# Seven chunks of a fourth output unit ahead of the first stage's last chunk, and the last attention shares turned after three chunks instead of six

## The chip, the cores and the metric

The kernel runs on one core of one Trainium2 chip. The metric is the device time of one execution in microseconds; the lower the better. All times below that name a place in the execution are microseconds from the start of the profiled span.

## The reference, cut to what matters

Two transformer-like blocks follow each other on a sequence of 512 positions with 1024 channels in float32. The change touches the end of the first block's mixing stage and the end of the second block's attention.

```python
# first block, one of 8 heads each for the recurrence (y_a) and the stick-breaking attention (y_b)
y_a = rg_lru(conv(xr), ...) * gelu(yr)
y_b = stick_breaking_attention(q, k, v)
mix = sigmoid(ga) * y_a + sigmoid(gb) * y_b      # [512, 1024]: 8 chunks of 128 channels, one a head
x = x + gt1 * (mix @ w_out)                      # 8 output units of 128 channels, each over 8 chunks
h2 = rmsnorm(x, norm2_g) * (1 + sc2) + sh2       # needs the sum of squares over all 1024 channels
# second block, latent attention, 8 heads
p = softmax(q @ k.T); o = p @ v                  # p is "the shares", 4 blocks of 128 queries
x = x + concat([o, pooled]) * silu(gate) @ w_out # a_out units: the half that reads o
```

## The kernel before, in words

Activations lie transposed: 128 channels on the partitions, 512 positions along the row. A *unit* is 128 output channels: up to eight chunks of 128 input channels, and three matmuls of 128x128 weights by 512 columns for each chunk (high weights by high input, high by low, low by high), since each float32 value is split into two parts, "hi" and "lo". `unit(kind, m, hi, lo, part=range(...))` issues some chunks of a unit on TensorE; the function starts at L715, and its three matmuls are L729 to L731.

Weights of a unit arrive by DMA in one of three `raw` buffers (L574). ScalarE copies them to the home's hi half (L1262, one instruction), and GpSimd subtracts to make the lo half in two instructions (L690, L695), after which the semaphore `w_split` is raised. There are three ordinary homes and two or three spare ones at a time. A home is used again only when the unit that read it before is finished (`unit_done`). Among the units of the first stage's output, `w_out` 0, 1 and 2 lie in ordinary homes 2, 0 and 1; `w_out` 3 and 4 in the two spare homes (seen in the trace as `qk_hl`); `w_out` 5, 6 and 7 take the homes of `w_out` 0, 1 and 2 again; then `ff_g` 0 takes that of `w_out` 3, `ff_v` 0 that of `w_out` 4, and `ff_g` 1 that of `w_out` 5.

TensorE's program is one list in a fixed order. At the end of the first stage it is: the gates of head 7, the turned weights of its attention (L898), `w_out` 0 over seven chunks, the attention products (`products`, L905), `w_out` 1 and 2 over seven chunks, then a wait for the eighth mixed chunk (`y_mixed`, raised by VectorE at L1984), the eighth chunk's matmuls for units 0 to 2 by the hi input (L993), then by the lo input (L997, after `mixed`, L1986), which finish these three units, and then units 3 to 6 whole. Unit 7 is done in two halves of 256 columns (L1016 to L1018). In its second half, before chunk 3, TensorE waits for the summed squares and turns them into a sum over channels:

```python
if i and k == 3:
    pe.wait_ge(x_summed, SUMS[0] + 6)
    nc.tensor.matmul(m_a[:, HALVES[0]], c_("ones"), sq_sum[:, HALVES[0]], start=True, stop=False)   # L1011
```

The squares come about as follows. VectorE adds a finished unit to `x` (L2059), ScalarE squares it (L1331), GpSimd adds the square to `sq_sum` (L651). ScalarE's program for this stretch is

```python
for m in range(7):
    split_ahead(UNIT[("w_out", m if m < 6 else 7)])   # L1262 for every home that is free by then
    act.wait_ge(res1_done, m + 1)
    x_square(0, m)                                    # L1331
```

and GpSimd's is in a fixed order too: the lo halves of `w_out` 5 and `w_out` 6, add 1, `w_out` 7, add 2, `ff_g` 0, add 3, `ff_v` 0, add 4, `ff_g` 1, add 5, add 6, `ff_v` 1. The lo half of `w_out` 5 can't begin before ScalarE has written its hi half, and that waits for the home of `w_out` 0 (L1257).

After the sum (L1011 and L1013) ScalarE takes the root (L1278, L1281), VectorE scales (L2073), ScalarE and VectorE make `h` hi and lo, and the next stage's first three units begin on TensorE (`trio`, L806 to L811).

At the end of the second attention TensorE runs `a_out` 0 over six chunks, the products of head 6, `a_out` 1 over six chunks, and then turns the four blocks of head 7's shares (`shares_turned(g, b)`, L1111, four transposes each). A block goes through one of two banks of PSUM; ScalarE copies it out (L1652) and VectorE subtracts (L2345, raises `pt_low`). `shares_turned(g, b)` waits for `pt_low` of the block two before it, and for the shares themselves (`p_ready`, GpSimd, L679). Between the blocks stand the seventh chunk of `a_out` 0 and of `a_out` 1. The seventh chunk of `a_out` 0 waits for `ya_tail` (VectorE, L2338).

Of the kernel before, what the change touches and what calls it, by code (L numbers as in the profile page):

```python
# [208 lines left out]
def build(nc, ada, weights, c_rows, params, consts, rg_w, x_t, positions, inv_counts, out_t):  # L209
    ctx = ExitStack()  # L210
    with ctx:
# [219 lines left out]
        def c_(name):  # L431
            a, n = CONST[name]
            return cst[:, a:a + n]
# [97 lines left out]
        def weights_of(n):  # L531

            hi, lo = home(PACK[n])
            cols = slice(WCOL[n], WCOL[n] + P * UNITS[n][2])
            return hi[:, cols], lo[:, cols]

        def psum_of(n):
            if BANK[n] > 4:
                return m_b
            return lin[:, BANK[n], :] if BANK[n] < 2 else big[:, BANK[n] - 2, :]  # L540
# [14 lines left out]
        def freed(n):  # L555
            kind, j, _ = UNITS[BEFORE[n]]
            return FREED[kind], 4 if kind == "ckv" else j + 1
# [156 lines left out]
        def _(pe):  # L714
            def unit(kind, j, hi, lo, ready=None, part=None):  # L715

                n = UNIT[(kind, j)]
                nk = UNITS[n][2]
                w_h, w_l = weights_of(n)
                if part is None or part[0] == 0:  # L720
                    pe.wait_ge(w_split, PACK[n] + 1)
                    if BEFORE[n] is not None:
                        f, v = freed(n)
                        pe.wait_ge(f, v)
                for k in part or range(nk):
                    if ready:
                        pe.wait_ge(*ready(k))
                    wh, wl = w_h[:, k * P:(k + 1) * P], w_l[:, k * P:(k + 1) * P]
                    nc.tensor.matmul(psum_of(n), wh, hi(k), start=(k == 0), stop=False)  # L729
                    nc.tensor.matmul(psum_of(n), wh, lo(k), start=False, stop=False)  # L730
                    last = nc.tensor.matmul(psum_of(n), wl, hi(k), start=False, stop=(k == nk - 1))  # L731
                if k == nk - 1:
                    last.then_inc(unit_done, 1)
# [22 lines left out]
            def YH(k):  # L756
                return y_hi[:, k]

            def YL(k):
                return y_lo[:, k]  # L760
# [130 lines left out]
            def weights_turned(g):  # L891

                pe.wait_ge(att_exp, g + 1)
                for of_bank in ((0,), (1, 3), (2,)):
                    for j in of_bank:
                        for b in range(j, TB):
                            to, of = COL[j] + (b - j) * P, COL[TB - 1 - b] + j * P
                            last = nc.tensor.transpose(big_f[:, to:to + P], att_a[:, of:of + P], c_("ident"))  # L898
                    last.then_inc(att_turned, 1)

            def products(g):

                for j in range(TB):
                    pe.wait_ge(att_done, 3 * g + (1, 2, 3, 2)[j])
                    last = nc.tensor.matmul(m_o[:, j * P:T], vtok[:, g % 2, j],  # L905
                                            att_b[:, COL[j]:COL[j] + KW[j]],
                                            start=(j == 0), stop=(j == TB - 1))
                last.then_inc(av_done, 1)
# [72 lines left out]
            pe.wait_ge(gate_r_read, HEADS)  # L981
            nc.tensor.matmul(m_a[:], rgw[:, 8 + g], A(S1["xr"], g), start=True, stop=True).then_inc(gates_done, 1)
            weights_turned(g)
            for m in range(3):
                unit("w_out", m, YH, YL, ready=None if m else lambda k: (mixed, k + 1), part=range(7))
                if m == 0:
                    products(g)
            pe.wait_ge(gates_read, HEADS)
            pe.wait_ge(y_mixed, HEADS + 1)
            for m in range(3):  # L990
                n = UNIT[("w_out", m)]
                for of in weights_of(n):
                    nc.tensor.matmul(psum_of(n), of[:, 7 * P:8 * P], YH(7), start=False, stop=False)  # L993
            pe.wait_ge(mixed, HEADS)
            for m in range(3):
                n = UNIT[("w_out", m)]
                nc.tensor.matmul(psum_of(n), weights_of(n)[0][:, 7 * P:8 * P], YL(7), start=False, stop=True)\  # L997
                    .then_inc(unit_done, 1)
            for m in range(3, 7):
                unit("w_out", m, YH, YL)  # L1000
            n = UNIT[("w_out", 7)]
            w_h, w_l = weights_of(n)
# [99 lines left out]
            def shares_turned(g, b):  # L1102

                q = 4 * g + b
                pe.wait_ge(vn_low, 8)
                if q - 1 > 0:
                    pe.wait_ge(pt_low, q - 1)
                pe.wait_ge(p_ready, q + 1)
                bank = (m_a, m_b)[q % 2]
                for j in range(TB):  # L1110
                    last = nc.tensor.transpose(bank[:, j * P:(j + 1) * P], p_sb[:, b, j * P:(j + 1) * P], c_("ident"))  # L1111
                last.then_inc(pt_done, 1)
# [22 lines left out]
            def latent_products(g):  # L1135

                pe.wait_ge(pt_low, 4 * g + 4)
                if g > 0:
                    pe.wait_ge(ya_scaled, g)
                own = slice((g % 4) * P, (g % 4 + 1) * P)  # L1140
                for j in range(TB):
                    vh, vl = vn_hi[g // 4][:, j, own], vn_lo[g // 4][:, j, own]
                    nc.tensor.matmul(m_o[:], vh, pt_hi[:, j], start=(j == 0), stop=False)
                    nc.tensor.matmul(m_o[:], vh, pt_lo[:, j], start=False, stop=False)
                    last = nc.tensor.matmul(m_o[:], vl, pt_hi[:, j], start=False, stop=(j == TB - 1))
                last.then_inc(pv_done, 1)
# [21 lines left out]
            g = HEADS - 1  # L1168
            unit("a_out", 0, YH, YL, part=range(6), ready=mixed_values)
            latent_products(g - 1)  # L1170
            unit("a_out", 1, YH, YL, part=range(6))
            shares_turned(g, 0)
            shares_turned(g, 1)
            unit("a_out", 0, YH, YL, part=range(6, 7), ready=mixed_values)
            shares_turned(g, 2)
            unit("a_out", 1, YH, YL, part=range(6, 7))
# [6 lines left out]
            for m in range(8):  # L1183
                unit("a_out", m, YH, YL, ready=None if m else mixed_values,
                     part=range(7, DK) if m < 4 else None)
# [1449 lines left out]
```

## Time and profile before

| | us |
|---|---|
| three runs | 1646.56, 1645.77, 1646.53; median 1646.53 |
| the profiled execution, its own time | 1646.32 |
| span of its profile | 1644.4 |
| TensorE busy | 1626.1 (99%) |
| GpSimd busy | 817.1 (50%) |
| mean granted TensorE clock | 0.998 of full speed |

The time outside the span is 1.9 us. A matmul's recorded duration overlaps that of the next, so starts are compared, not ends: successive matmuls of 512 columns start about 0.23 us apart. A number in brackets behind a row is the engine's idle time ahead of it, with what ended it. "xN" merges N instructions in a row, and the second number is then the time of all of them.

### The profile page before, as it was taken

The page shows a single profiled execution, that of the slowest core. Times are in us where ns is not written, and L with a number is a line of the kernel's source. Part 1 is how long each engine was busy: PE and PEld are TensorE (multiplying, and loading weights), DVE is VectorE, ACT ScalarE, POOL GpSimd, SP SyncE. Part 2 cuts the span into 40 slices and gives each one's busy share as a digit, 9 for nine tenths or more (in the row PEclk, how much of TensorE's full clock was granted, in tenths as well). Part 3 has the DMA queues.
Part 4 walks back from the last instruction along what each step waited for, and adds up shares of the span by engine and source line. Part 5 has one row for each costly group of instructions (what it writes and reads, how often), then busy time and mean ns, then how long its engine had stood idle before and what let it go on. Part 6 is the DMA issues. An engine that isn't in the chain of part 4 may idle for free.

```text
span 1644.4 us, 19632 instructions
## 1 busy us (share of the span) xinstructions
PE 1626.1 (99%) x7244; PEld 1322.2 (80%) x7244; DVE 994.6 (60%) x1214; ACT 813.5 (49%) x1025; POOL 817.1 (50%) x590
## 2 busy tenths in 40 slices
PE   8999999999999999999999999999999999999997
PEld 4777777787888888888888888788888888888885
DVE  7588888889488358335526775665347553255541
ACT  5666666667454244333443343677454444244443
POOL 5345444454755545445565644455483443543424
PEclk9999999999999999999999999999999999999999
DMA  9434433333422332333232322211232222231212
GB/s 379 157 115 141 141 116 128 129 103 106 130 90 90 103 102 92 119 98 102 90 98 82 103 87 70 67 39 52 64 129 64 65 90 65 91 97 57 90 53 76
DMA packets 47039, 167.35 MB, mean 102 GB/s; under 512 B 5216, under 2 KB 5344, under 8 KB 46688
## 3 DMA queue, kind: packets, MB, share of 16 engines
q1 hardware_dynamic: 46944, 166.09, 30.6%
q8 instruction: 58, 0.95, 0.2%
q14 instruction: 37, 0.30, 0.1%
HBM read 163.98 MB, written 2.10 MB: 101 GB/s over the span
## 4 chain that ended last, share of the span: by engine, by line
PE 90%; DVE 7%; ACT 1%; issue 1%; DMA 1%; POOL 0%; POOLq 0%; DVEq 0%; ACTq 0%
PE lin L729 16%; PE lin L731 16%; PE lin L730 16%; PE big L730 7%; PE big L729 7%; PE big L731 7%; PE m_bo L747 1%; PE m_bo L745 1%; PE m_bo L746 1%; DVE scr L1912 1%; DVE tmp L1949 1%; PE big L1225 1%; PE big L1224 1%; PE big L1223 1%; PE big L887 1%
## 5 line engine op out<-in xcount | busy, mean ns | idle before, releaser
L690 POOL TENSOR_TENSOR w_lo<-raw,w_hi 128x512 fp32r<-128x512 f32 x197 | 285.2, 1448 | 591.9 <-ACT w_hi L1262 591.7
L729 PE MATMUL lin<-h_hi,w_hi 128*128 128x512 f32 x888 | 350.9, 395 | 0.0
L731 PE MATMUL lin<-h_hi,w_lo 128*128 128x512 f32 x888 | 345.9, 390 | 0.0
L730 PE MATMUL lin<-h_lo,w_hi 128*128 128x512 f32 x888 | 345.9, 389 | 0.0
L695 POOL TENSOR_TENSOR w_lo<-raw,w_hi 128x512 fp32r<-128x512 f32 (+1 forms) x206 | 305.6, 1484 | 14.0 <-ACT w_hi L1262 14.0
L1262 ACT ACTIVATE w_hi<-raw 128x1024 fp32r<-128x1024 f32 (+2 forms) x206 | 214.6, 1042 | 191.1 <-PE m_bo L747 47.0
L729 PEld LDWEIGHTS lin<-h_hi,w_hi 128*128 128x128 f32 x888 | 166.7, 188 | 36.4 <-issue 2.2
L730 PEld LDWEIGHTS lin<-h_lo,w_hi 128*128 128x128 f32 x888 | 166.8, 188 | 36.2 <-issue 2.2
L731 PEld LDWEIGHTS lin<-h_hi,w_lo 128*128 128x128 f32 x888 | 166.7, 188 | 35.1
L690 POOL TENSOR_TENSOR qk_hl<-raw,qk_hl 128x512 fp32r<-128x512 f32 x43 | 59.8, 1391 | 113.6 <-ACT qk_hl L1262 113.5
L729 PE MATMUL lin<-y_hi,w_hi 128*128 128x512 f32 x258 | 100.8, 391 | 0.0
L731 PE MATMUL lin<-y_hi,w_lo 128*128 128x512 f32 x258 | 100.4, 389 | 0.0
L730 PE MATMUL lin<-y_lo,w_hi 128*128 128x512 f32 x258 | 100.4, 389 | 0.0
L1262 ACT ACTIVATE qk_hl<-raw 128x1024 fp32r<-128x1024 f32 (+1 forms) x44 | 46.3, 1053 | 54.8 <-DVE x L2181 33.0
L730 PE MATMUL big<-h_lo,qk_hl 128*128 128x512 f32 x184 | 71.6, 389 | 0.0
L729 PE MATMUL big<-h_hi,qk_hl 128*128 128x512 f32 x184 | 71.6, 389 | 0.0
L731 PE MATMUL big<-h_hi,qk_hl 128*128 128x512 f32 x184 | 71.6, 389 | 0.0
L2163 DVE SCALAR_TENSOR_TENSOR scr<-big,par,scr 128x511 f32<-128x511 f32 (+1 forms) x58 | 43.5, 750 | 45.4 <-ACT scr L1540 34.2
L695 POOL TENSOR_TENSOR qk_hl<-raw,qk_hl 128x512 fp32r<-128x512 f32 x44 | 62.3, 1416 | 0.1
L679 POOL TENSOR_TENSOR scr<-scr,small 128x512 f32<-128x512 f32 x32 | 32.3, 1042 | 52.6 <-DVE small L2386 52.6
L731 PEld LDWEIGHTS lin<-y_hi,w_lo 128*128 128x128 f32 x258 | 48.4, 188 | 10.1
L730 PEld LDWEIGHTS lin<-y_lo,w_hi 128*128 128x128 f32 x258 | 48.4, 188 | 10.0
(572 smaller groups left out, 3514.4 us busy)
## 6 DMA issues: line engine op xcount, KB each, us to landing
raw<-weights SPq DMA_DIRECT2D x245, 512.0 KB, 3.5
slab<-ada SPq DMA_DIRECT2D x32, 512.0 KB, 4.6
scr<-ada SPq DMA_DIRECT2D x16, 512.0 KB, 8.6
raw<-weights SPq DMA_DIRECT2D x10, 256.0 KB, 2.8
x<-x_t SPq DMA_DIRECT2D x4, 512.0 KB, 5.3
out_t<-scr SPq DMA_DIRECT2D x8, 256.0 KB, 2.6
raw<-weights SPq DMA_DIRECT2D x4, 448.0 KB, 3.3
rgw<-rg_w SPq DMA_DIRECT2D x1, 1024.0 KB, 6.9
```

Of the source, the lines that this page charges most:

```text
L679: nc.gpsimd.tensor_tensor(p_sb[:, b], p_sb[:, b], sm(STAT + 4 + b).broadcast_to([P, T]), ALU.mult).then_inc(p_ready, 1)
L690: nc.gpsimd.tensor_tensor(lo[:, 0:4 * P], raw[:, s, 0:4 * P], hi[:, 0:4 * P].bitcast(F32), ALU.subtract).then_inc(w_half, 1)
L695: nc.gpsimd.tensor_tensor(lo[:, at:w], raw[:, s, at:w], hi[:, at:w].bitcast(F32), ALU.subtract).then_inc(w_split, 1)
L729: nc.tensor.matmul(psum_of(n), wh, hi(k), start=(k == 0), stop=False)
L730: nc.tensor.matmul(psum_of(n), wh, lo(k), start=False, stop=False)
L731: last = nc.tensor.matmul(psum_of(n), wl, hi(k), start=False, stop=(k == nk - 1))
L745: nc.tensor.matmul(rv_bank[b], hh, wh, start=(k == 0), stop=False)
L746: nc.tensor.matmul(rv_bank[b], hh, wl, start=False, stop=False)
L747: last = nc.tensor.matmul(rv_bank[b], hl, wh, start=False, stop=(k == DK - 1))
L887: last = nc.tensor.matmul(big_f[:, COL[i]:COL[i] + KW[i]], A(S1["q"], g)[:, b * P:(b + 1) * P], A(S1["k"], g)[:, 0:KW[i]], start=True, sto ...
L1262: nc.scalar.activation(home(e)[0][:, 0:WIDTH[e]], raw[:, s, 0:WIDTH[e]], ACT.Copy).then_inc(w_high, 1)
L2163: v.scalar_tensor_tensor(out=o[:, s:T], in0=psum_of(n)[:, 0:T - s], scalar=p_("ffn_conv_w", 48 * (2 - s) + half + c), in1=o[:, s:T], op0=M ...
```

## The change

The first part of the change lets `w_out` 3 join the units that run over seven chunks before the wait for the eighth mixed chunk, and has its eighth chunk done with the others'. The second part puts the turning of the last head's share blocks 0 and 1 behind three chunks of `a_out` 1; the other three chunks follow them.

```diff
             weights_turned(g)
-            for m in range(3):
+            for m in range(4):
                 unit("w_out", m, YH, YL, ready=None if m else lambda k: (mixed, k + 1), part=range(7))
                 if m == 0:
                     products(g)
             pe.wait_ge(gates_read, HEADS)
             pe.wait_ge(y_mixed, HEADS + 1)
-            for m in range(3):
+            for m in range(4):
                 n = UNIT[("w_out", m)]
                 for of in weights_of(n):
                     nc.tensor.matmul(psum_of(n), of[:, 7 * P:8 * P], YH(7), start=False, stop=False)
             pe.wait_ge(mixed, HEADS)
-            for m in range(3):
+            for m in range(4):
                 n = UNIT[("w_out", m)]
                 nc.tensor.matmul(psum_of(n), weights_of(n)[0][:, 7 * P:8 * P], YL(7), start=False, stop=True)\
                     .then_inc(unit_done, 1)
-            for m in range(3, 7):
+            for m in range(4, 7):
                 unit("w_out", m, YH, YL)
...
             unit("a_out", 0, YH, YL, part=range(6), ready=mixed_values)
             latent_products(g - 1)
-            unit("a_out", 1, YH, YL, part=range(6))
+            unit("a_out", 1, YH, YL, part=range(3))
             shares_turned(g, 0)
             shares_turned(g, 1)
+            unit("a_out", 1, YH, YL, part=range(3, 6))
             unit("a_out", 0, YH, YL, part=range(6, 7), ready=mixed_values)
             shares_turned(g, 2)
             unit("a_out", 1, YH, YL, part=range(6, 7))
```

## Rows read from the trace of the kernel before

**Rows 1.** The page: busy time of engines, and the chain that ended last.
```profile
PE 1626.1 (99%) x7244; PEld 1322.2 (80%) x7244; DVE 994.6 (60%) x1214; ACT 813.5 (49%) x1025; POOL 817.1 (50%) x590
...
PE 90%; DVE 7%; ACT 1%; issue 1%; DMA 1%; POOL 0%; POOLq 0%; DVEq 0%; ACTq 0%
```

**Rows 2.** Whom TensorE waited for: us in total, times, longest.
```profile
PE lin L854 <- POOL h_lo L656: 3.5, 3, 1.4
...
PE lin L993 <- DVE y_hi L1984: 0.3, 1, 0.3
```

**Rows 3.** Timeline of TensorE at the first wait: start, duration, instruction, [idle before].
```profile
412.84 0.39 PE L729 MATMUL big<-y_hi,w_hi 128*128 128x512 f32 x1
...
417.37 0.39 PE L731 MATMUL big<-y_hi,w_lo 128*128 128x512 f32 x1
418.07 0.47 PE L993 MATMUL lin<-y_hi,w_hi 128*128 128x512 f32 x1 [0.32 <-DVE y_hi L1984]
...
419.52 0.61 PE L997 MATMUL lin<-y_lo,w_hi 128*128 128x512 f32 x2
...
420.20 0.39 PE L729 MATMUL big<-y_hi,qk_hl 128*128 128x512 f32 x1
```

**Rows 4.** Timeline of ScalarE in the same stretch.
```profile
420.87 0.64 ACT L1331 ACTIVATE sq_sum<-x 128x512 f32<-128x512 f32 x1 [7.78 <-DVE x L2059]
421.54 1.06 ACT L1262 ACTIVATE w_hi<-raw 128x1024 fp32r<-128x1024 f32 x1
```

**Rows 5.** Timeline of GpSimd: lo halves of w_out 3 to 7, then adds of squares.
```profile
415.85 1.29 POOL L695 TENSOR_TENSOR qk_hl<-raw,qk_hl 128x512 fp32r<-128x512 f32 x1
422.68 1.29 POOL L690 TENSOR_TENSOR w_lo<-raw,w_hi 128x512 fp32r<-128x512 f32 x1 [5.54 <-ACT w_hi L1262]
...
442.68 2.75 POOL L651 TENSOR_TENSOR sq_sum<-sq_sum,sq_act 128x512 f32<-128x512 f32 x2
445.39 1.28 POOL L690 TENSOR_TENSOR w_lo<-raw,w_hi 128x512 fp32r<-128x512 f32 x1
```

**Rows 6.** Timeline of TensorE in unit 7's second half and at the next stage's start.
```profile
445.92 0.59 PE L1011 MATMUL m_a<-sq_sum,cst 128*128 128x256 f32 x2
446.35 0.59 PE L1013 MATMUL m_a<-sq_act,cst 128*128 128x256 f32 x2
...
448.56 0.59 PE L1021 MATMUL m_a<-sq_sum,cst 128*128 128x256 f32 x2
449.22 0.36 PE L806 MATMUL big<-h_hi,qk_hl 128*128 128x256 f32 x1
```

**Rows 7.** Timeline of TensorE around the turned shares.
```profile
1165.74 0.39 PE L729 MATMUL lin<-y_hi,cq_lo 128*128 128x512 f32 x1
...
1169.83 0.60 PE L1111 MATMUL m_a<-cst,scr 128*128 128x128 f32 x4
...
1171.16 0.40 PE L731 MATMUL lin<-y_hi,cq_hi 128*128 128x512 f32 x1
1172.00 0.63 PE L1111 MATMUL m_a<-cst,scr 128*128 128x128 f32 x4 [0.44 <-issue]
```

**Rows 8.** ScalarE and VectorE for block 0, and GpSimd's four scaled blocks.
```profile
1170.51 0.60 ACT L1652 ACTIVATE scr_r<-m_a 128x512 fp32r<-128x512 f32 x1 [3.09 <-PE m_a L1111]
...
1171.21 0.69 DVE L2345 TENSOR_TENSOR scr_r<-m_a,scr_r 128x512 fp32r<-128x512 f32 x1 [2.99 <-ACT scr_r L1652]
...
1161.13 4.04 POOL L679 TENSOR_TENSOR scr<-scr,small 128x512 f32<-128x512 f32 x4 [6.30 <-DVE small L2386]
```

**Rows 9.** Windows: stretch, its length, busy time of each engine, granted clock, DMA.
```profile
28.00:32.00 4.00, 2.62 (x12) 1.62 (x11) 3.85 (x7) 2.75 (x4) 3.25 (x3) 1.00 1.03 408
1634.00:1635.00 1.00, 0.73 (x2) 0.00 (x0) 0.00 (x0) 0.17 (x1) 0.00 (x0) 1.00 0.00 0
...
1637.00:1638.00 1.00, 0.00 (x0) 0.00 (x0) 0.93 (x3) 0.00 (x0) 1.00 (x1) 0.54 0.12 45
1638.00:1639.00 1.00, 0.00 (x0) 0.00 (x0) 0.96 (x2) 0.00 (x0) 1.00 (x2) 0.50 0.90 332
```

## The prediction

> **What bounds the kernel now.** I read the page first. TensorE is busy 99% of the span and makes 90% of the chain that ended last [rows 1], so a gap that appears on TensorE, or goes away, moves the end almost one for one. The view of whom TensorE waited for shows how little is left: its largest sum is 3.5 us, in the first stage's start, and the wait at the eighth mixed chunk, which the first part of the change aims at, is 0.3 us [rows 2]. Then I read the timelines of the two places, TensorE's first and the other engines' beside it. The reader is to look in them for two things: what the gap really costs in starts of matmuls, and which engine has no idle time in the stretch that follows.
>
> **The first wait goes.** Unit 2's 21 matmuls start from 412.84 to 417.37, so they are 4.53 / 20 = 0.2265 us apart [rows 3]. The next would start at 417.60; it starts at 418.07, 0.47 late. The six matmuls by the hi input then take 1.45 instead of 1.36, so the restart costs 0.09 more. With unit 3's seven chunks in between, TensorE is busy for 21 x 0.2265 = 4.76 us more before it asks for the eighth chunk, from 417.60 to 422.36, and VectorE's hi value is there by 418.0. Unit 3's weights are there as well: the spare homes' lo halves end with the instruction at 415.85, that of unit 4, ending 417.14, and unit 3's ends before it starts [rows 5]. TensorE's own list is thereby 0.56 us shorter: unit 4 starts at 422.36 + 12 x 0.2265 = 425.08, where unit 3 would have ended at 420.20 + 24 x 0.2265 = 425.64 [rows 3], and so does every unit up to unit 7 begin 0.56 us sooner.
>
> **What is late next.** The added work stands not only ahead of the wait but ahead of the end of units 0 to 2. Unit 0's last matmul started at 419.52 [rows 3]. It now comes behind 21 matmuls of unit 3 and eight, no longer six, by the hi input: 422.36 + 8 x 0.2265 = 424.17, which is 4.65 us later. On unit 0 hang the first residual and square, and home 2, in which the weights of unit 5 are wanted. ScalarE's square starts 1.35 us after that matmul, its copy for unit 5 0.67 us later, and GpSimd 1.14 us behind that [rows 3 to 5]. These become 425.52, 426.19 and 427.33. Unit 5's lo half, two instructions of 1.29 at most, then ends by 429.91. TensorE asks for it at 425.08 + 5.44 = 430.52, so that the weights themselves are in time by 0.6 us.
>
> The sum of squares isn't. From 422.68 to 445.39 GpSimd goes through 18 instructions (twelve halves of weights, six adds) with no idle time beyond 0.2 us: two adds at 442.68 take 2.75 instead of some 2.54, since the last waits for its square [rows 5]. TensorE takes the sum at 445.92 [rows 6], 0.5 us after the last add has ended at 445.43. That was the whole slack. Shifted, the 18 instructions run from 427.33 for 22.71 us, or 22.50 when the last square is early: its inputs are residuals of units 5 and 6, which come 0.56 us sooner. The last add then ends at about 449.87. TensorE arrives at 445.36 and waits 4.5 us, to about 449.95. I looked for an earlier bound and found none: the weights of `ff_g` and `ff_v` that stand between the adds are loaded when the lo half three entries before is done, 5 us or more ahead, and stay hidden under the same GpSimd chain.
>
> Against before, the sum starts 449.95 - 445.92 = 4.03 us later, and a restart costs some 0.1 more, as at 418.07: 4.1 us. What follows hangs on this matmul link by link: root, scaling, h hi and lo, the trio, whose first matmul at 449.22 already comes 0.2 us later than TensorE could have issued it [rows 6]. So all of it shifts by 4.1, and the next stages are bound by TensorE and give nothing back. The 0.56 us saved ahead of this wait is already in the sum (445.92 counts, not 445.36). Bounds for this term: GpSimd's pace is known from the mean of 18 instructions, 1.26 us from start to start, and I allow 0.3 us either way: 3.8 to 4.4, unless the order is otherwise than I read it.
>
> **The clock.** A second cost is not in the timing of any matmul of this trace. At the span's end the granted clock goes from 1.00 to 0.54 in the microsecond from 1637 and is 0.50 behind it; the levels 1.00 and 0.50 are 2.4 and 1.2 GHz. The mean of 0.54 puts the fall at about 1637.1. The last matmuls are recorded into the microsecond from 1634, of which TensorE is busy 0.73: the fall comes some 2.4 us after them [rows 9]. In the stretch from 28 to 32, with TensorE busy for 2.62 of 4 us, the clock stayed at 1.00. The new gap without a matmul is 4.4 us in one piece, far nearer to the first case, and I take a fall as likely. Its price isn't in a row, as no matmul runs at 0.50. It is bounded from below by nothing (the clock returns as soon as work does), and from above by half of the time that it stays low, at most about the length of the gap again: 4.4 / 2 = 2.2 us. The work behind the gap is dense, with only 0.2 us of waiting to absorb any of it. I take 1.3.
>
> The Trainium skill ("TensorE: Matmul & The Clock Gate", section "Why this matters for your kernels") advises against idle gaps of some microseconds between bursts of matmuls, since TensorE goes back to half clock. By it a fall is to be expected here; without a fall the sum is 1650.0, the first rival below. The end of this trace agrees with it, and no matmul here shows what it costs.
>
> **The second part.** `shares_turned(g, 2)` starts at 1172.00, though the last matmul before it started at 1171.16 and the next could start at 1171.39: 0.61 late [rows 7]. It waits for block 0's lo part, made by VectorE from 1171.21 to 1171.90, behind ScalarE's copy, 0.68 us after the transposes' start [rows 8]. Moved ahead by 9 matmuls, the transposes of block 0 start at 1165.74 + 9 x 0.2265 = 1167.78, and its lo part is done at 1169.85. TensorE comes to block 2 at the same 1171.39, as it has issued the same matmuls with as many changes from transposes to units and back, and doesn't wait. The shares are ready: GpSimd ends all four blocks at 1165.17 [rows 8]. The seventh chunk of `a_out` 0 keeps its place in time. Block 3 and the products keep their distance to block 2. Nothing new is late: -0.61 us, kept to the end. Bounds: 0 if another wait ends there, -0.7.
>
> **Sum.** 4.1 + 1.3 - 0.6 = +4.8 us. On the profiled execution that is 1646.32 + 4.8 = 1651.1. The median of the runs lies 0.21 above it, and I forecast against the median: 1651.3.
>
> **Rivals.**
> 1. *The clock doesn't fall.* All else as above: 4.1 - 0.6 = +3.5, 1650.0. For it speaks that a gap of this length doesn't occur amid the kernel's work. Against it, the fall 2.4 us behind the last matmul at the end.
> 2. *The sum of squares is not what TensorE waits for; both gains stay.* 1646.53 - 0.56 - 0.61 = 1645.4, within 0.2%. This is the other side. It would need GpSimd's adds to end no later than 445.3, that is, less than 18 us for 18 instructions that take 22.5 now, or GpSimd's run not hanging on unit 0's home. For it speaks only that GpSimd is idle half of the span. Against it, the 5.54 us of idle time that ended with ScalarE's copy for unit 5, and none after it [rows 5]. The place decides from a lateness of 0.5 us on; 4.65 is forecast.
> 3. *The clock stays low well into the trio, or the late start leaves the stage's chain further behind.* TensorE's work from the sum to the trio, 448.56 + 0.59 - 445.92 = 3.2 us, would take twice as long, and so would the trio's first microseconds: +3.2 instead of 1.3, 1653.2.
> 4. *The first part as forecast, the second a wait exchanged for another.* +5.4, 1651.9; inside the range.
>
> **How the numbers follow.** Differences of under 0.2% (3.3 us) are about what a measurement of this kernel can't tell from no change. My forecast, stall and fall of the clock, has 0.65, with its own range 1650.5 to 1652.5 (clock price 0.6 to 2.0, rival 4 in it). Rival 1 has 0.20, rival 3 0.08 and rival 2 0.04; other things 0.03. The range that leaves out no more than 2 in 10 has to take in rival 1's 1650.0 with 0.3 below it, and the longer low clock: 1649.7 to 1653.2. Rival 1 lies at +3.5, hardly beyond 0.2%, so half of it counts as slower. Slower: 0.65 + 0.10 + 0.08 + 0.01 = 0.84; the same: 0.10 + 0.04 + 0.01 = 0.15; faster: 0.01, as no case gains more than 1.2 us.
>
> **What would show it.** In the profile after: no idle time ahead of L993; GpSimd's first half for unit 5 at about 427.3 behind some 10 us of idle time; L1011 at about 450.0 with 4.4 us idle ahead of it, released by GpSimd's L651; a slice or window there with a granted clock below 1.00; matmuls of 256 columns 0.24 apart instead of 0.12 for a few microseconds; the first L806 5 us later than 449.22; block 2 of the shares without idle time ahead of it. The prediction is wrong if L1011 starts without idle time, or if L1011's releaser is ScalarE or a weight load.

## The result and the profile after

The changed kernel takes 1652.0 us (median of 7 runs, 1651.01 to 1652.37), the one before 1646.37 (median of 7, 1645.77 to 1647.13): 5.6 us more, ratio 1.0033 with a 95% interval of 1.0023 to 1.0042. The profiled execution took 1652.37, its span is 1650.3 against 1644.4. The forecast was 1651.3 and slower.

TensorE's waits in the changed kernel (us in total, times, longest): one is new at the top, and that at the eighth mixed chunk [rows 2] is gone, as is the one at the turned shares.

```profile
PE m_a L1011 <- POOL sq_sum L651: 4.5, 1, 4.5
PE lin L854 <- POOL h_lo L656: 3.5, 3, 1.4
```

TensorE's timeline at the old wait, to be held against [rows 3]. Unit 3 begins at 417.60 without a gap, and the first `L997`, which ends unit 0, comes at 424.18 instead of 419.52.

```profile
417.38 0.39 PE L731 MATMUL big<-y_hi,w_lo 128*128 128x512 f32 x1
417.60 0.39 PE L729 MATMUL big<-y_hi,qk_hl 128*128 128x512 f32 x1
...
422.36 0.39 PE L993 MATMUL lin<-y_hi,w_hi 128*128 128x512 f32 x1
...
424.18 0.61 PE L997 MATMUL lin<-y_lo,w_hi 128*128 128x512 f32 x2
...
425.08 0.39 PE L729 MATMUL big<-y_hi,qk_hl 128*128 128x512 f32 x1
```

GpSimd's timeline, to be held against [rows 5]. The idle time ahead of unit 5's lo half has grown from 5.54 to 10.19 us, and behind it there is none, as before. (Line numbers of ScalarE and VectorE are one higher in this kernel.)

```profile
427.33 1.30 POOL L690 TENSOR_TENSOR w_lo<-raw,w_hi 128x512 fp32r<-128x512 f32 x1 [10.19 <-ACT w_hi L1263]
...
447.30 2.67 POOL L651 TENSOR_TENSOR sq_sum<-sq_sum,sq_act 128x512 f32<-128x512 f32 x2
449.92 1.26 POOL L690 TENSOR_TENSOR w_lo<-raw,w_hi 128x512 fp32r<-128x512 f32 x1
```

TensorE's timeline at the sum of squares, to be held against [rows 6]: 4.50 us of idle time, then matmuls of 256 columns 0.21 us apart instead of 0.12, and the trio's first matmul at 455.58 instead of 449.22.

```profile
445.24 0.28 PE L1018 MATMUL lin<-y_hi,w_lo 128*128 128x256 f32 x1
450.02 1.22 PE L1011 MATMUL m_a<-sq_sum,cst 128*128 128x256 f32 x2 [4.50 <-POOL sq_sum L651]
451.03 1.06 PE L1013 MATMUL m_a<-sq_act,cst 128*128 128x256 f32 x2
...
453.81 0.41 PE L1016 MATMUL lin<-y_hi,w_hi 128*128 128x256 f32 x1
454.02 0.41 PE L1017 MATMUL lin<-y_lo,w_hi 128*128 128x256 f32 x1
...
455.58 0.73 PE L806 MATMUL big<-h_hi,qk_hl 128*128 128x256 f32 x1
456.15 0.28 PE L807 MATMUL big<-h_hi,qk_hl 128*128 128x256 f32 x1
```

Windows of one microsecond there (the columns are those of [rows 9]; the granted clock is the third number from the end). It goes from 1.00 to 0.50, that is from 2.4 to 1.2 GHz, and is back in the last row.

```profile
448.00:449.00 1.00, 0.00 (x0) 0.00 (x0) 0.00 (x0) 0.41 (x1) 0.86 (x2) 1.00 0.52 131
449.00:450.00 1.00, 0.00 (x0) 0.00 (x0) 0.00 (x0) 0.01 (x1) 1.00 (x2) 0.65 0.94 373
450.00:451.00 1.00, 0.98 (x2) 0.84 (x3) 0.00 (x0) 0.00 (x0) 1.00 (x1) 0.50 0.73 281
...
455.00:456.00 1.00, 1.00 (x5) 0.82 (x4) 0.57 (x2) 0.02 (x1) 0.00 (x0) 0.50 0.17 66
456.00:457.00 1.00, 1.00 (x10) 0.97 (x8) 0.93 (x3) 0.39 (x1) 0.00 (x0) 0.93 0.00 0
```

From the two means of 0.65 and 0.93 the clock was low from about 449.3 to 456.1.

The first matmul of 512 columns behind all this, in the kernel before and in the changed one:

```profile
458.56 0.40 PE L806 MATMUL big<-h_hi,qk_hl 128*128 128x512 f32 x1
```
```profile
465.10 0.40 PE L806 MATMUL big<-h_hi,qk_hl 128*128 128x512 f32 x1
```

At the second place TensorE goes from `a_out` 0's seventh chunk to share block 2 without idle time [rows 7].

```profile
1172.31 0.39 PE L729 MATMUL lin<-y_hi,cq_lo 128*128 128x512 f32 x1
...
1174.35 0.60 PE L1111 MATMUL m_a<-cst,scr 128*128 128x128 f32 x4
1174.79 0.60 PE L1111 MATMUL m_bo<-cst,scr 128*128 128x128 f32 x4
...
1177.77 0.40 PE L731 MATMUL lin<-y_hi,cq_hi 128*128 128x512 f32 x1
1178.00 0.60 PE L1111 MATMUL m_a<-cst,scr 128*128 128x128 f32 x4
```

The differences add up. The sum of squares (L1011) starts 450.02 - 445.92 = 4.10 late. The trio starts 6.36 late and its first matmul of 512 columns is at 465.10 instead of 458.56, 6.54 late; what came on top of 4.10 is 2.44. `a_out` 1 begins 6.57 late (1172.31 against 1165.74), block 2 is 6.00 late, so the second part has given back 0.57, and the span's end is 5.9 late.

### The profile page after: what moved, and what is told of

The parts are those of the page before. It is cut to its first block, busy times and chain, and to the rows that moved or that the text cites. A ratio compares the mean times of both kernels' runs of the same rounds, so it can differ in the third digit from the quotient of the medians.

```text
span 1650.3 us, 19632 instructions
## 1 busy us (share of the span) xinstructions
PE 1628.4 (99%) x7244; PEld 1324.9 (80%) x7244; DVE 994.2 (60%) x1214; ACT 813.0 (49%) x1025; POOL 817.6 (50%) x590
## 4 chain that ended last, share of the span: by engine, by line
PE 92%; DVE 4%; POOL 1%; ACT 1%; issue 1%; DMA 1%; POOLq 0%; DVEq 0%; ACTq 0%
PE lin L729 16%; PE lin L730 16%; PE lin L731 16%; PE big L730 7%; PE big L729 7%; PE big L731 7%; PE m_bo L745 1%; PE m_bo L747 1%; PE m_bo L746 1%; PE big L887 1%; PE m_bo L905 1%; PE big L1224 1%; PE big L1226 1%; PE big L1225 1%; PE big L898 1%
## 5 line engine op out<-in xcount | busy, mean ns | idle before, releaser
L729 PEld LDWEIGHTS lin<-y_hi,w_hi 128*128 128x128 f32 x258 | 48.4, 188 | 10.0
```

## The experiments

What the two theories disagree on is whether the lateness of unit 0's end, through GpSimd's fixed order, is the whole mechanism, and whether the low clock adds to it or is hidden. Each comparison is with runs of the kernel before on the same chip, whose median is given.

### Each part alone

`e1_part1_only` is the changed kernel with the second part taken back; `e2_part2_only` is the kernel before with the second part alone.

```diff
 e1: -            unit("a_out", 1, YH, YL, part=range(3))
     +            unit("a_out", 1, YH, YL, part=range(6))
                  shares_turned(g, 0)
                  shares_turned(g, 1)
     -            unit("a_out", 1, YH, YL, part=range(3, 6))
```

> Only the four w_out units over seven chunks. My theory: this part holds the whole loss, and the second part's gain of 0.6 us is missing, so 0.6 us above the changed kernel, about 1652.6 (before plus 6.2); L1011 at 450.0 with 4.5 us of idle time ahead of it, released by GpSimd. Rival: the loss comes from the second stage's reordering, then this kernel is at 1645.8, as before less 0.56.

> Only the turned shares moved. My theory: 0.6 us below before, 1645.8, block 2 of the shares with no idle time ahead of it. Rival: the wait moves to another place of the stage, then the time is that of before, 1646.4.

The first part alone took a median of 1653.06 against 1646.61 before, +6.45, ratio 1.0039 (1.0026 to 1.0051). The second part alone took 1645.88, -0.73, ratio 0.9995 (0.9986 to 1.0004), which by its interval can't be told from no change; the trace can tell it: `e2`'s timeline has no idle time ahead of block 2, at 1171.51, where before it had 0.44 us [rows 7].

```profile
1167.86 0.60 PE L1111 MATMUL m_a<-cst,scr 128*128 128x128 f32 x4
1168.30 0.60 PE L1111 MATMUL m_bo<-cst,scr 128*128 128x128 f32 x4
1171.51 0.60 PE L1111 MATMUL m_a<-cst,scr 128*128 128x128 f32 x4
```

So the whole loss sits in the first part. In `e1` TensorE's waits have the new one of 4.5 us for L651, as in the changed kernel, and beside it the old one at the shares:

```profile
PE m_a L1111 <- issue: 0.4, 1, 0.4
```

Two things in `e1`'s profile are not as in the changed kernel's. The sum is at 451.06, not at the 450.0 expected, because this execution was 1.0 us late before the changed place: one of its first matmuls starts at 11.61 instead of 10.58, and unit 2's last matmul already starts at 418.41 instead of 417.38. From that matmul to the sum both take 32.6 us. And the clock is low for half as long, from about 451.4, just after TensorE has begun again, to about 454.8:

```profile
451.06 0.95 PE L1011 MATMUL m_a<-sq_sum,cst 128*128 128x256 f32 x2 [4.51 <-POOL sq_sum L651]
...
465.15 0.40 PE L806 MATMUL big<-h_hi,qk_hl 128*128 128x512 f32 x1
```
```profile
451.00:452.00 1.00, 0.94 (x3) 0.82 (x4) 0.00 (x0) 0.00 (x0) 1.00 (x2) 0.69 0.77 299
...
454.00:455.00 1.00, 1.00 (x7) 1.00 (x7) 0.88 (x2) 0.51 (x1) 0.00 (x0) 0.61 0.43 49
```

From the sum to the first matmul of 512 columns it takes 14.09 us, where the changed kernel took 15.08 and the kernel before 12.64 (445.92 to 458.56).

### The clock apart from the wait

`e3_clock_kept` is the changed kernel with matmuls in the idle time whose result nobody reads; they go to a bank that is free there.

```diff
                     if i and k == 3:
+                        keep_clock(19, lin[:, 0], ones_r[:], y_hi[:, 0])
                         pe.wait_ge(x_summed, SUMS[0] + 6)
```

> The changed kernel with 19 matmuls of 512 columns, whose result nobody reads, in the place of TensorE's idle time ahead of the sum of squares (19 x 0.2265 = 4.3 us from 445.4 to 449.7). The wait itself stays as long. My theory, that the loss of 5.6 us has two terms (4.1 for the wait, less 0.6 for the second part, and some 2.4 for a granted clock at half): L1011 again at 450.0, granted clock 1.00 throughout, 2.4 us below the changed kernel, 1649.6. Rival: the low clock is hidden behind the chain of root, scaling and h, then the time is that of the changed kernel, 1652.0.

It took 1649.91 against 1646.61, +3.30, ratio 1.0021 (1.0012 to 1.0030). TensorE's timeline shows the 19 matmuls, the sum at the same 450.02, and the trio at 453.42 instead of 455.58; the granted clock from 449 to 456 was 1.00.

```profile
445.24 4.59 PE L784 MATMUL lin<-y_hi,ones_r 128*128 128x512 f32 x19
450.02 0.70 PE L1012 MATMUL m_a<-sq_sum,cst 128*128 128x256 f32 x2 [0.19 <-POOL sq_sum L651]
453.42 0.36 PE L806 MATMUL big<-h_hi,qk_hl 128*128 128x256 f32 x1
...
462.77 0.40 PE L806 MATMUL big<-h_hi,qk_hl 128*128 128x512 f32 x1
```

The two terms are thus parted by a run. Wait: 1649.91 - 1645.88 (`e2`, same chip) = 4.03 us. Clock: 2.3 us by the spans of the profiled executions (1650.3 and 1648.0), 5.63 - 3.30 = 2.3 by the medians, each against its own before. The way from the sum to the first matmul of 512 columns, which leaves out all that happened earlier in an execution, gives the same: 15.08 - 12.75 = 2.33. By this measure the low clock cost 14.09 - 12.75 = 1.34 in `e1`'s profiled execution. So its price is not one number: it went with how long TensorE worked at the low clock, 6.1 us in the one and 3.4 in the other. The rival, a low clock hidden behind root and scaling, falls.

### How many chunks may stand ahead

`e4_one_chunk` and `e5_four_chunks` have the second part, and one or four chunks of `w_out` 3 ahead of the wait. The eighth chunk's matmuls stay with three units.

```diff
+            unit("w_out", 3, YH, YL, part=range(1))        # range(4) in e5
             pe.wait_ge(gates_read, HEADS)
...
-            for m in range(3, 7):
+            unit("w_out", 3, YH, YL, part=range(1, DK))
+            for m in range(4, 7):
                 unit("w_out", m, YH, YL)
```

> The second part, and of the first only one chunk of w_out 3 ahead of the wait, its other seven behind. Three matmuls (0.68 us) cover the wait of 0.47 us, and unit 0 ends at 417.60 + 0.68 + 6 x 0.2265 = 419.64 instead of 419.52, 0.12 late. My theory (what costs is the lateness of unit 0's end beyond GpSimd's slack of 0.5 us): no idle time ahead of L993, and at most 0.1 us ahead of L1011, before less 0.5 less 0.6, 1645.3. Rival: any chunk of unit 3 ahead of the wait costs more than it covers (a bank or a weight load), then at or above 1646.

> As the kernel with one chunk of w_out 3 ahead of the wait, but with four of its chunks ahead. Unit 0's last matmul then starts at 417.60 + 12 x 0.2265 + 1.36 = 421.68 instead of 419.52, 2.16 late. My theory: the last add ends 2.0 late, L1011 starts at 447.4 with some 2.0 us of idle time ahead of it, so before plus 1.5 less 0.6, 1647.5 if the clock stays at full speed; if it falls after 2 us as well, up to 2 us more. Rival, that the loss comes with the seventh chunk or with the eighth one's grouping: no idle time ahead of L1011 and 1645.3.

With one chunk: 1645.80 against 1646.61, ratio 0.9994 (0.9986 to 1.0003). In the trace the wait ahead of L993 is gone, and at the sum about 0.2 us of waiting is left: it starts 0.33 behind the matmul before it, where 0.12 is usual. The sum starts 0.53 sooner than in the kernel before and the trio 0.42; this execution was already 0.17 ahead at unit 2's last matmul (417.20 against 417.37), so the place itself gave 0.36 and 0.25.

```profile
445.39 0.70 PE L1013 MATMUL m_a<-sq_sum,cst 128*128 128x256 f32 x2
...
448.80 0.36 PE L806 MATMUL big<-h_hi,qk_hl 128*128 128x256 f32 x1
```

With four chunks: 1648.07 against 1646.33, ratio 1.0011 (1.0002 to 1.0019), 2.06 us of idle time at the sum, as forecast; its profiled execution, at a granted clock of 1.00 from 445 to 458, took 1647.78.

```profile
447.90 0.70 PE L1013 MATMUL m_a<-sq_sum,cst 128*128 128x256 f32 x2 [2.06 <-POOL sq_sum L651]
```

One, four and seven chunks thus give 0.2, 2.06 and 4.50 us of idle time: the loss follows the lateness of unit 0's end, chunk by chunk. Against the second part alone (1645.88), the one chunk that covers the wait is worth 0.3 us in the traces (from unit 2's last matmul to the first of 512 columns 40.94 us in `e4` and 41.23 in `e2`) and nothing that the medians can show.

### GpSimd late, with no matmul moved

`e7_gpsimd_late` has the second part and TensorE's first stage as before. GpSimd does the first lo half of `w_out` 5 four times more. No result changes. (The count that the last output transfers wait for on `out_pool` is raised by four; that line is left out here.)

```diff
+                if e == PACK[UNIT[("w_out", 5)]]:
+                    for i in range(4):
+                        nc.gpsimd.tensor_tensor(lo[:, 0:4 * P], raw[:, s, 0:4 * P], hi[:, 0:4 * P].bitcast(F32),
+                                                ALU.subtract).then_inc(out_pool, 1)
+                        pool.wait_ge(out_pool, i + 1)
```

> TensorE's order at the first stage's end as before the change, with only the second part of it; but GpSimd computes the first lo half of w_out 5 four times more, each with a wait for the one before, so that its run begins some 5.4 us late without any matmul moved. My theory: last add at 450.7, L1011 at 450.8 instead of 445.9 with some 4.8 us of idle time, and the clock falls: 1645.9 + 4.9 + 2.4 = 1653.2. Rival (the loss comes from the order of the matmuls or from the banks, GpSimd's lateness is absorbed): 1645.9.

It took 1652.82 against 1646.33, ratio 1.0038 (1.0026 to 1.0051). The loss of the changed kernel is there again without its cause on TensorE. From the sum to the first matmul of 512 columns it takes 14.78 us (450.84 to 465.62), so the low clock cost 2.03 here.

```profile
422.67 5.40 POOL L691 TENSOR_TENSOR w_lo<-raw,w_hi 128x512 fp32r<-128x512 f32 x4 [5.57 <-ACT w_hi L1268]
```
```profile
450.84 1.22 PE L1016 MATMUL m_a<-sq_sum,cst 128*128 128x256 f32 x2 [4.77 <-POOL sq_sum L651]
```

### GpSimd's order

`e6_adds_first` is the changed kernel with GpSimd's adds 5 and 6 ahead of its work for `ff_g` 1.

```diff
-                    if e == PACK[UNIT[f]] + 6 + (NR + SPARE if r < 3 else NR):
+                    if r == 0 and e == PACK[UNIT[f]] + 5 + NR + SPARE:
+                        add_square(r, 5)
+                        add_square(r, 6)
+                    if r > 0 and e == PACK[UNIT[f]] + 6 + (NR + SPARE if r < 3 else NR):
                         add_square(r, 6)
...
-                    if 1 <= m < 6:
+                    if 1 <= m < (6 if r else 5):
                         add_square(r, m)
```

> The changed kernel with GpSimd's adds 5 and 6 ahead of its two instructions for ff_g 1 and not behind them. My theory (TensorE waits for GpSimd's run in its fixed order): the last add 2.5 us sooner, L1011 at 447.5 with 2.1 us of idle time, and the trio's weights still in time; the changed kernel less 2.5, less the 2.4 of the clock if that doesn't fall in a gap of 2.1 us: 1647.1, else 1649.5. Rival (the last add waits for its square and thus for ScalarE, not for GpSimd's order): L1011 stays near 450.

It took 1648.34 against 1646.33, ratio 1.0013 (1.0004 to 1.0022). The sum starts at 447.49, as forecast, 2.5 us sooner than in the changed kernel: what TensorE waits for is GpSimd's order, not ScalarE's last square.

```profile
447.49 0.70 PE L1014 MATMUL m_a<-sq_sum,cst 128*128 128x256 f32 x2 [2.28 <-POOL sq_sum L651]
```

The time is 1.2 us above the 1647.1 expected. Two things were open then. The runs lie in two groups, six from 1647.78 to 1648.34 and five from 1649.00 to 1649.32, and the mean granted clock is 0.998 in all of the first and 0.997 in all of the second. (In `e5` it is likewise 0.997 in the five slowest runs, from 1648.14, and 0.998 in the other six.) And in the profiled execution, of the first group (1647.91), VectorE's first h lo half takes three times as long as the next ones: GpSimd's work for `ff_v` 1 runs until 452.4, as in the changed kernel, but VectorE's first half is now due earlier and falls into it. From the sum to the first matmul of 512 columns it takes 13.27 us here, at full clock, and 12.75 in `e3` and `e5`: 0.5 of the 1.2 us. VectorE's and GpSimd's timelines:

```profile
451.22 1.45 DVE L2085 SCALAR_TENSOR_TENSOR h_lo<-tmp,small,h_hi 128x256 fp32r<-128x256 f32 x1
...
453.22 0.48 DVE L2085 SCALAR_TENSOR_TENSOR h_lo<-tmp,small,h_hi 128x256 fp32r<-128x256 f32 x1
...
451.11 1.28 POOL L698 TENSOR_TENSOR w_lo<-raw,w_hi 128x512 fp32r<-128x512 f32 x1
```

### Short gaps filled

`e8_four_chunks_filled` and `e9_adds_first_filled` are `e5` and `e6` with nine unread matmuls in the gap, put as in `e3`.

```diff
+                        keep_clock(9, lin[:, 0], ones_r[:], y_hi[:, 0])
```

> The kernel with four chunks of w_out 3 ahead of the wait, with nine matmuls that nobody reads in the idle time ahead of the sum of squares (9 x 0.2265 = 2.0 us). My theory: the runs of the unfilled kernel spread from 1647.0 to 1648.8 because the clock falls in some of them after a gap of 2.1 us and in others not; filled, all lie near the lowest, median 1647.3, spread within 0.6 us. Rival (another cause of the spread): median 1648.1, and the spread stays.

> The kernel with GpSimd's adds 5 and 6 ahead of ff_g 1, with nine matmuls that nobody reads in the idle time ahead of the sum of squares. My theory: the unfilled kernel's runs fall into 1647.8 to 1648.3 and 1649.0 to 1649.3 by the clock; filled, only the lower group is left, median 1647.8. What remains above the 1647.1 first expected is GpSimd's work for ff_g 1 and ff_v 1, which now runs beside VectorE's first h lo half and stretches it from 0.48 to 1.45 us. Rival: the median stays at 1648.3 with both groups.

| | unfilled, us | filled, us | median before of the filled runs |
|---|---|---|---|
| four chunks (`e5`, `e8`) | 1646.96 to 1648.82, median 1648.07 | 1647.03 to 1647.76, median 1647.57 | 1646.41 |
| adds first (`e6`, `e9`) | 1647.78 to 1649.32, median 1648.34 | 1647.86 to 1648.96, median 1648.21 | 1646.41 |

For four chunks it came nearly as expected: ratio 1.0006 (0.9997 to 1.0015), a spread of 0.7 instead of 1.9 us (0.6 was expected), the lowest runs the same, the median 0.3 above the expectation. For the adds first only in part: the group above 1649 is gone, but two of eleven runs (1648.81 and 1648.96) lie above the rest, the median moved by 0.1, ratio 1.0010 (1.0001 to 1.0020), and the median is 0.4 above the expectation. VectorE's long first half is there as well (1.45 us), with the same 13.27 us. So a gap of 2.1 to 2.3 us seems to bring the clock down in some executions and not in others. That is not shown: it rests on the groups and on mean clocks of 0.998 and 0.997, which are one step of rounding apart. Runs of 0.997 also occur where no such gap is, among them three of the four fastest of `e4` (1645.13, 1645.25, 1645.31), and the two high runs of `e9` have 0.998. No execution with a low clock after such a short gap was profiled.

## Why the prediction was right

- *The first wait goes, TensorE's list is 0.56 us shorter.* Right. Unit 4 starts at 425.08, to the hundredth as worked out, and no matmul waits ahead of L993.
- *What is late next.* Right, the term that makes the loss. Unit 0's last matmul at 424.18 (forecast 424.17), ScalarE's copy at 426.19 (426.19), GpSimd at 427.33 (427.33), the last add's end at about 449.9 (449.87), the sum at 450.02 (449.95), its wait 4.5. The sum was to be 4.03 late, and the restart to cost 0.1 more; it is 4.10 late, and the restart costs 0.1 (12.75 us from the sum to the first matmul of 512 columns in `e3`, 12.64 before). The term of 4.1 is thus 4.2 in the trace; by runs it is 4.03 (`e3` against `e2`). `e5` and `e4` show that its size follows the number of chunks, `e7` that GpSimd's lateness alone suffices, `e6` that GpSimd's order sets it.
- *The clock.* The mechanism was right, the term too small: 1.3 in the forecast with bounds of 0 and 2.2, some 2.3 measured in the changed kernel. The upper bound had said that the clock stays low at most about as long as the gap; no row showed that, and 1.3 was a choice between the bounds. The clock fell only at 449.3, near the gap's end, and stayed low for 6.8 us. TensorE worked in it from 450.0 to 456.1; half of these 6.1 us would be 3.05. Why it was 2.33 can be read by holding the starts against those of `e3`. At full clock TensorE waits some 0.4 us for `h` ahead of the trio's first matmul (it starts 0.65 behind L1022, where 0.25 is enough behind L1014) and 0.2 inside the trio; at half clock these waits are gone. That is 0.6, and the forecast had allowed 0.2. The last 0.1 goes with the matmuls of 256 columns, which start 0.21 instead of 0.12 us apart, less than double. How long the clock stays low is what the forecast had no row for, and it varied: 1.34 in `e1`'s execution, which is the forecast's 1.3, 2.03 in `e7`'s, 2.33 in this one. What sets the moment of the fall stays open. The Trainium skill's advice against such gaps ("TensorE: Matmul & The Clock Gate", "Why this matters for your kernels") holds here, with a granted clock of 0.50 behind a gap of 4.50 us, and `e3` now gives it a price.
- *The second part.* Right: forecast -0.61; in the traces of the changed kernel and of `e2` block 2 comes 0.57 sooner, counted from the start of `a_out` 1, and by runs it is -0.73 alone and about -0.8 beside the first part (6.45 - 5.63), both less certain than the trace.
- *Sum.* 4.1 + 2.3 - 0.7 = 5.7 against 5.6 measured. The forecast of +4.8 fell short by the clock's term, and the time still lay inside its range because the range had room for a longer low clock.
- *Rivals.* Rival 2, in which both gains stay, had its turning point at 0.5 us of lateness; `e4`, with 0.12, lies on the one side and waits only 0.2 us at the sum, `e5`, with 2.16, on the other. Rival 1 is what `e3` builds, at 1649.91 where 1650.0 was worked out. Rival 3, a clock that stays low well into the trio at +3.2, came true in part: in the changed kernel the clock returned at 456.1, half a microsecond into the trio, in `e1` and `e7` before it, and the measured 2.3 lies about half way between the forecast's 1.3 and its 3.2.

## What to carry to other kernels

If a wait of half a microsecond on the busiest engine is to be covered, then with just enough work to cover it (here that was worth 0.3 us in the traces and nothing that the medians show); what is put ahead of a wait is also put ahead of everything that finishes behind it. Before such a move, follow the late thing (here the end of the first unit) through the homes and buffers that it frees to the next engine whose queue has no idle time left, and compare with that queue's slack, which was 0.5 us here though GpSimd is idle half of the span. A gap of 4.5 us on TensorE cost its length here and 1.3 to 2.3 us of slow clock behind it; matmuls that nobody reads bought back the cost of the slow clock.

## What the runs showed of the hardware beyond that

- How long after the last matmul's end the granted clock fell differs from execution to execution: 3.8 us in the changed kernel (445.5 to 449.3), 4.8 us in `e1` (446.55 to about 451.4, when TensorE was at work again), 2.8 us in `e7` (to about 448.9), and some 2.4 us at the end of the kernel before [rows 9]. It returned 6.1 us after TensorE had begun again in the changed kernel, 3.7 us in `e1` (451.06 to about 454.8) and 4.9 us in `e7` (450.84 to about 455.8), whose windows are:

```profile
448.00:449.00 1.00, 0.00 (x0) 0.00 (x0) 0.00 (x0) 0.00 (x0) 1.00 (x2) 0.96 0.00 0
...
455.00:456.00 1.00, 1.00 (x7) 1.00 (x6) 0.00 (x0) 0.55 (x2) 0.00 (x0) 0.62 0.95 373
```

- At half clock, matmuls of 256 columns start 0.21 us apart instead of 0.12, which is less than double.
- VectorE's `h` lo half of 256 columns took 1.45 instead of 0.48 us beside one of GpSimd's subtractions in `e6` and `e9`, while its residual adds, which read PSUM, kept 0.75 to 0.77 us beside GpSimd's adds and subtractions in the changed kernel. That the overlap is the cause was not tested by itself.
